# Merging the two softmax maps of a differential pair before they are transposed

## What is computed

```
def differential_attention(q1, q2, k1, k2, v, lam):
    ...
        s1 = jnp.where(causal, jnp.einsum('bqhd,bkhd->bhqk', qa, k1).astype(jnp.float32), -jnp.inf)
        s2 = jnp.where(causal, jnp.einsum('bqhd,bkhd->bhqk', qb, k2).astype(jnp.float32), -jnp.inf)
        attn = jax.nn.softmax(s1, axis=-1) - lam * jax.nn.softmax(s2, axis=-1)
        return jnp.einsum('bhqk,bkhe->bqhe', attn.astype(v.dtype), v)
    ...
o_d = rmsnorm(o_d, diff_norm) * (1.0 - lambda_init)
```

## Time and profile before

| | value |
|---|---|
| median of 3 runs | 2049.18 us (2048.17 to 2049.33) |
| profiled execution | 2048.13 us, its span 2046.2 us |
| busy share of the span | PE 99%, PEld 83%, DVE 79%, ACT 49%, POOL 3% |
| granted TensorE clock | 0.999 of full speed over the span |
| DMA | 376.64 MB, mean 184 GB/s |

### The profile page before, as it was taken

One profiled execution on the slowest core, in us unless ns is written; L12 is line 12 of the kernel. 1 busy time (PEld: TensorE's weight loads), 2 busy tenths in 40 slices (PEclk: granted clock), 3 DMA queues, 4 the chain that ended last, 5 costly groups with the idle time before them and its releaser, 6 DMA issues.

```text
span 2046.2 us, 26929 instructions
## 1 busy us (share of the span) xinstructions
PE 2035.4 (99%) x9638; PEld 1693.0 (83%) x9638; DVE 1619.2 (79%) x2701; ACT 1003.5 (49%) x1192; POOL 67.9 (3%) x87
## 2 busy tenths in 40 slices
PE   9999999999999999999999999999999999999998
PEld 7888888888888888888888889888888888888887
DVE  7888767888887866787888888758888888777887
ACT  5445554444544455454454446355444544665443
POOL 0000100000000010000001000010000000020000
PEclk9999999999999999999999999999999999999999
DMA  6754544555475453465547554234555654434553
GB/s 234 285 189 165 191 147 157 211 200 186 184 257 201 168 197 147 149 213 198 185 167 257 188 185 164 85 123 185 187 198 185 218 196 178 175 141 170 191 197 111
DMA packets 54335, 376.64 MB, mean 184 GB/s; under 512 B 6560, under 2 KB 6704, under 8 KB 9584
## 3 DMA queue, kind: packets, MB, share of 16 engines
q1 hardware_dynamic: 51264, 364.67, 49.3%
q0 software_dynamic: 2560, 10.55, 1.6%
q10 hardware_dynamic: 432, 0.33, 0.0%
HBM read 374.47 MB, written 1.05 MB: 184 GB/s over the span
## 4 chain that ended last, share of the span: by engine, by line
PE 98%; DVE 1%; ACT 1%; issue 0%; DMA 0%; POOL 0%; POOLq 0%; SPq 0%; DVEq 0%; ACTq 0%
PE bank L1654 30%; PE bank L1656 30%; PE bank L1655 30%; PE bank L1663 1%; PE bank L2096 1%; PE bank L2104 1%; PE bank L1877 1%; PE bank L2174 0%; PE bank L1851 0%; PE bank L2175 0%; PE bank L2176 0%; PE bank L1886 0%; DVE w_lo L937 0%; PE bank L1897 0%; PE bank L1899 0%
## 5 line engine op out<-in xcount | busy, mean ns | idle before, releaser
L937 DVE TENSOR_TENSOR w_lo<-w_raw,w_hi 128x2048 fp32r<-128x2048 f32 x344 | 787.5, 2292 | 185.0 <-ACT w_hi L465 116.3
L1654 PE MATMUL bank<-w_hi,xt_hi 128*128 128x512 f32 x1888 | 744.6, 394 | 1.6 <-DVE w_lo L937 1.0
L1656 PE MATMUL bank<-w_hi,xt_lo 128*128 128x512 f32 x1888 | 736.0, 390 | 0.0
L1655 PE MATMUL bank<-w_lo,xt_hi 128*128 128x512 f32 x1888 | 735.2, 389 | 0.0
L994 DVE STREAM_TRANSPOSE mix<-hid 32x128 f32<-32x128 f32 x1408 | 425.8, 302 | 18.3
L1654 PEld LDWEIGHTS bank<-w_hi,xt_hi 128*128 128x128 f32 x1888 | 354.7, 188 | 75.9 <-issue 2.9
L1656 PEld LDWEIGHTS bank<-w_hi,xt_lo 128*128 128x128 f32 x1888 | 354.4, 188 | 74.8
L1655 PEld LDWEIGHTS bank<-w_lo,xt_hi 128*128 128x128 f32 x1888 | 354.8, 188 | 71.2 <-issue 0.2
L465 ACT ACTIVATE w_hi<-w_raw 128x2048 fp32r<-128x2048 f32 x176 | 335.3, 1912 | 147.5 <-PE bank L1656 139.0
L539 ACT ACTIVATE w_hi<-w_raw 128x2048 fp32r<-128x2048 f32 x168 | 320.8, 1910 | 150.8 <-PE bank L1656 150.8
L1654 PE MATMUL bank<-w_hi,ht_hi 128*128 128x512 f32 x608 | 236.7, 389 | 0.0
(11 more groups left out here) (274 smaller groups left out, 1333.9 us busy)
## 6 DMA issues: line engine op xcount, KB each, us to landing
w_raw<-weights_dram SPq DMA_DIRECT2D x345, 1024.0 KB, 4.8
mix<-a_b_gate_dram POOLq DMA_DIRECT2D x4, 1024.0 KB, 14.9
mix<-a_pool_mean_dram POOLq DMA_DIRECT2D x2, 768.0 KB, 7.8
x<-x_dram SPq DMA_DIRECT2D x4, 256.0 KB, 6.4
w_raw<-weights_dram SPq DMA_DIRECT2D x4, 256.0 KB, 6.1
out_dram<-xn SPq DMA_DIRECT2D x3, 256.0 KB, 2.4
mix<-a_pool_w_dram POOLq DMA_DIRECT2D x2, 256.0 KB, 2.9
mix<-g_ret_dram POOLq DMA_DIRECT2D x1, 512.0 KB, 9.6
```

What stands on the lines that cost most here:

```text
L937: nc.vector.tensor_tensor(w_lo[s][:, :], w_raw[s][:, :], w_hi[s][:, :].bitcast(F32), ALU.subtract).then_inc(lo_done, 1)
L1654: nc.tensor.matmul(out, a_hi, b_hi, start=start, stop=False)
L1655: nc.tensor.matmul(out, a_hi, b_lo, start=False, stop=False)
L1656: return nc.tensor.matmul(out, a_lo, b_hi, start=False, stop=stop)
```

## The change

The two maps of a pair are merged after the exponentials and before the transposes. A new DVE step `merge_pair(r)` forms, in place in the first map, map 2r minus lambda times (row sum 1 / row sum 2) times map 2r+1. There is then one turn, one `take_probs` and one `values` a pair. The remaining scale, one over the first row sum, is applied by ACT when it takes the result out of bank 7: `take_pair` moves from DVE to ACT. The eight maps get four buffers `maps` of their own (in `B`, 1536 columns). The dilated maps keep `probs`, and the counts of turns and products go up by one a pair instead of two.

The orders are rewritten too. In pieces 6 to 9 DVE does both `soft` of a pair, then `w_lo` (`ahead`), then `merge_pair`. ACT does `take_pair` and `square_head` of an earlier pair, both exponentials, then `w_hi` (`ahead`), then `take_probs`. On PE the turn of pair r stands in the hooks (7,0), (8,0), (9,0), (10,0) and its product with the values in (7,1), (8,1), (9,1), (10,1). The scores stay in (5,1), (6,1), (7,1) and (8,1).

```
 ScalarE, dil_diff
+                def take_pair(r):
+                    act.wait_ge(pv_done, g0 + r + 1)
+                    for tt in range(TT):
+                        ins = nc.scalar.activation(d4[:, tt, r], bank[7][:, tt * 256:tt * 256 + P], ACT.Copy, scale=expsum[:, 1, tt, 2 * r:2 * r + 1])
+                    ins.then_inc(o_ready, 1)
...
+                    if 8 <= p < 11:
+                        take_pair(p - 8)
+                        square_head(p - 8)
+                    if 6 <= p < 10:
+                        for m in (2 * (p - 6), 2 * (p - 6) + 1):
+                            exp_map(g0 + m, m, diff_map(m))
                     ahead(n0 + p)
...
-                    for step in steps_of(p, 6, 1):
-                        if 2 <= step < 10:
-                            take_probs(g0 + step - 2)
-                        if step < 8:
-                            exp_map(g0 + step, step)
-                        if step in (5, 7, 9):
-                            square_head((step - 5) // 2)
+                    if 7 <= p < 11:
+                        take_probs(g0 + p - 7)
                     if p == 10:
                         turned_qk(c0 + 2, "cqt", 4, B)
+                        take_pair(3)
                         square_head(3)
 VectorE, dil_diff
-                def take_pair(h):
...
+                def merge_pair(r):
+                    dve.wait_ge(exp_done, g0 + 2 * r + 2)
+                    i = 2 * r
                     link(nc.vector.reciprocal(expsum[:, 1, :, i:i + 2], expsum[:, 0, :, i:i + 2]))
                     second = expsum[:, 1, :, i + 1]
+                    link(nc.vector.scalar_tensor_tensor(out=second, in0=second, scalar=lam[:, 5:6], in1=expsum[:, 0, :, i], op0=ALU.mult, op1=ALU.mult))
+                    for tt, cols in enumerate((slice(0, P), slice(P, 3 * P))):
+                        ins = nc.vector.scalar_tensor_tensor(out=diff_map(i)[:, cols], in0=diff_map(i + 1)[:, cols],
+                                                             scalar=expsum[:, 1, tt, i + 1:i + 2], in1=diff_map(i)[:, cols],
+                                                             op0=ALU.mult, op1=ALU.add)
+                    ins.then_inc(maps_merged, 1)
...
                     if 6 <= p < 10:
-                        soft(g0 + 2 * p - 11, 0.125, B["mask"])
+                        soft_diff(2 * (p - 6))
+                        soft_diff(2 * (p - 6) + 1)
                     if p not in (11, last):
                         ahead(n0 + p)
+                    if 6 <= p < 10:
+                        merge_pair(p - 6)
 TensorE, dil_diff
+                def turn_merged_pair(r):
+                    pe.wait_ge(maps_merged, r + 1)
+                    turn_probs(g0 + r, diff_map(2 * r))
...
-                    if 2 <= step < 10:
-                        turn_probs(g0 + step - 2)
-                    if 0 <= step < 8 and step % 2 == 0:
+                    if step % 2 and 3 <= step < 10:
+                        turn_merged_pair((step - 3) // 2)
+                    if step % 2 == 0 and 0 <= step < 8:
                         diff_scores(step)
-                    if 3 <= step < 11:
-                        diff_values(step - 3)
+                    if step % 2 == 0 and 4 <= step < 11:
+                        diff_values((step - 4) // 2)
```

More of the change, by code:

```diff
@@ L647, in pool_attn @@
                         if step < 8:
-                            exp_map(g0 + step, step)
+                            exp_map(g0 + step, step, probs_of(g0 + step))
                     if p == 13 or p == 16:
@@ L1376, in rotate, with soft_diff, soft_dil @@
                     rope(heads(B[name], w), heads(B["rot"], w), tables[:, 0], tables[:, 1], w).then_inc(qk_ready, 1)
[L1378 to L1381 removed]
+                def merge_pair(r):
+                    dve.wait_ge(exp_done, g0 + 2 * r + 2)
+                    i = 2 * r
                     link(nc.vector.reciprocal(expsum[:, 1, :, i:i + 2], expsum[:, 0, :, i:i + 2]))
                     second = expsum[:, 1, :, i + 1]
[L1384 to L1391 removed]
+                    link(nc.vector.scalar_tensor_tensor(out=second, in0=second, scalar=lam[:, 5:6], in1=expsum[:, 0, :, i], op0=ALU.mult, op1=ALU.mult))
[4 more added lines that the diff above has]
+                    ins.then_inc(maps_merged, 1)
+                def soft_diff(m):
+                    if m >= 4:
+                        dve.wait_ge(pt_done, g0 + m // 2 - 1)
+                    soft(g0 + m, 0.125, B["mask"], diff_map(m))
+                def soft_dil(m):
+                    dve.wait_ge(pt_done, g0 + m + 3)
+                    soft(g0 + 8 + m, DIL_SCALE, B["mask_dil"], probs_of(g0 + 8 + m))
                 def lambda_sums():
@@ L1442, in dil_diff @@
                     for step in steps_of(p, 6, 1):
-                        if step < 8 and step % 2 == 0:
-                            soft(g0 + step, 0.125, B["mask"])
-                        if step in (4, 6, 8, 10):
-                            take_pair((step - 4) // 2)
                         if step in (6, 8, 10):
@@ L1457, in dil_diff @@
                         pair_low(bt0[k], 6, first_half)
-                        soft(g0 + 8, DIL_SCALE, B["mask_dil"])
-                        soft(g0 + 9, DIL_SCALE, B["mask_dil"])
+                        soft_dil(0)
+                        soft_dil(1)
                         pair_low(bt0[k] + 1, 7, second_half)
@@ L1573, in pool_attn @@
                         if step < 8:
-                            soft(g0 + step, 0.125, A["mask"])
+                            if g0 + step >= 2:
+                                dve.wait_ge(pt_done, g0 + step - 1)
+                            soft(g0 + step, 0.125, A["mask"], probs_of(g0 + step))
                         if step == 6:
@@ L2336, in diff_scores, with diff_values, turn_dil @@
                     scores_of_pair(g0 + m, mapped("qa")[:, m // 2], mapped("dkt")[:, m // 2])
-                def diff_values(m):
-                    values(g0 + m, m % 2, 2, [dv[:, tt, (m // 2) * P:(m // 2 + 1) * P] for tt in range(TT)], r0 + m // 2)
+                def turn_merged_pair(r):
+                    pe.wait_ge(maps_merged, r + 1)
+                    turn_probs(g0 + r, diff_map(2 * r))
+                def diff_values(r):
+                    values(g0 + r, 0, 2, [dv[:, tt, r * P:(r + 1) * P] for tt in range(TT)], r0 + r)
+                def turn_dil(m):
+                    pe.wait_ge(exp_done, g0 + 8 + m + 1)
+                    turn_probs(g0 + 4 + m, probs_of(g0 + 8 + m))
                 def dil_scores(m):
@@ L2344, in dil_values @@
                 def dil_values(m):
-                    values(g0 + 8 + m, m % 2, 2, [cv[:, tt, m * P:(m + 1) * P] for tt in range(TT)], r0 + 4 + m // 2)
+                    values(g0 + 4 + m, m % 2, 2, [cv[:, tt, m * P:(m + 1) * P] for tt in range(TT)], r0 + 4 + m // 2)
                 def with_tile(p, tt):
```

66 lines of the change are left out of this document (31 added, 35 removed).

## The result

The changed kernel takes 2052.4 us (median of 20 runs, 2051.8 to 2053.9) beside 2049.1 us of the kernel before (20 runs, 2048.1 to 2049.7). The ratio is 1.0017, interval 1.0012 to 1.0023: 2.5 to 4.7 us slower. Forecast was 2052.1.

The account below looks back on a forecast made before the run. PE bounds the kernel (98% of the chain), but its 4.04 us saving meets 3.96 of holds, plus 0.7 for norms and 2.35 for the port: 2051.1 from the profiled run, 2052.1 us on the median's scale, range 2049.0 to 2055.0.

Parts of the forecast that it names:

- PE's saving: On PE, four turns and four products fewer, 4.48 us, of which at most 4.04 us counts in the time.
- The ring: DVE and ACT wait on each other: merge, both soft, exponential, w_hi, w_lo, 8.54 us a piece; holds PE 3.96 us.
- The merge: On DVE, each merge_pair adds 1.14 us of pitch: reciprocal and small op 0.47, large ops 0.27 and 0.40.
- The norm of pairs 0 and 1: In hook (11,0), PE held 0.7 us because w_hi 12 stands behind take_pair 2 on ACT; hook +0.6 us later.
- The port: POOL's rotation of cq locks DVE out of SBUF during merge 1, which ends 2.35 us late, and PE with it.
- L378 has a wait of its own on POOL: At merge 1, POOL's first 1024-column op waits for L376, so both large merge ops may go ahead of it.
- the first rival: At merge 1, POOL's L378 gets in between merge instructions, 2.4 us more, kernel 2054.5 (with L380 2056.9); chance 0.27.
- The sum: Whole kernel: 2048.13 - 4.04 + 3.96 + 0.7 + 2.35 gives 2051.1, on the median's scale 2052.1 us, +2.95.
- The clock: On PE, a granted clock below 1.00 in a hold of over 2 us would make the forecast wrong.

Follow-up runs that it names:

- experiment 8: Changed kernel with merge_pair ahead of w_lo, w_hi 12 ahead of take_pair 2, and POOL's rotation of cq started by w_lo 9 and 10; 2044.71 us, ratio 0.9981.
- experiment 2: Changed kernel without POOL's rotation of cq, one 8-column instruction in place of the four; 2049.36 us, ratio 1.0001.
- experiment 3: Changed kernel with DVE's merge_pair ahead of the w_lo of its piece, POOL's rotation left in place; 2048.99 us, ratio 1.0002.
- experiment 4: experiment 1 with ACT's take_probs of pieces 7 to 9 ahead of both exponentials and w_hi; 2048.07 us, ratio 0.9997.
- experiment 6: experiment 4 with one more DVE instruction of 128x256 on an unread buffer behind each merge; 2053.32 us, ratio 1.0023.
- experiment 7: experiment 4 with ACT's take_pair 2 and its squares behind w_hi 12 instead of ahead of it; 2047.78 us, ratio 0.9998.
- experiment 5: Changed kernel with POOL's two 1024-column operations waiting until merge 1 is done, the two 512-column ones still meeting it; 2050.05 us, ratio 1.0008.
- experiment 1: Changed kernel with POOL's rotation of cq held back until merge 1 is done, its last instruction until merge 2; 2049.43 us, ratio 1.0003.

## Why the prediction came out, and where it didn't

**PE's saving, 4.04 us: right.** 36 matmuls fewer, and a turn or a product costs what the rows said. In experiment 8 cq's turn stands 3.67 us earlier in the stage than before, with one hold of 0.51 ahead of it; in experiment 2 it stands 0.26 us earlier, with holds of 3.92. Both make 4.18.

**The ring, 8.54 us a piece: right.** The merges start at 1788.96 (pair 0), 1797.47 (pair 1) and later 1809.92 and 1818.50: 8.51 and 8.58 us apart where POOL doesn't come in. Without POOL the three holds are 0.76, 0.93 and 2.23 us, 3.92 in all for 3.96 forecast. Experiments 3, 4 and 6 show that it is a ring: moving PE's meeting point moves the hold, lengthening it by 0.45 lengthens a turn from 8.50 to 8.96, and putting the merge ahead of `w_lo` shortens it to 7.39 us.

**The merge, 1.14 us: right.** The reciprocal starts at 1809.92 and the next step after the merge at 1811.05, 1.13 us. The two large ops take 0.75 together; the slower rate of the Trainium skill ("Vector Engine (DVE) Microarchitecture Reference", section 7) for two SBUF sources that are not bf16 does not show in any undisturbed merge. The sum would have been 1.2 us too high by it.

**The norm of pairs 0 and 1, +0.6 us: mechanism right, size off.** The hold is there (0.65, in experiment 2 0.64), and experiment 7 takes it away in the place named, `w_hi` 12 behind `take_pair` 2. But the forecast's +0.6 also had in it that saving and ring nearly cancel, -0.08, and they left -0.26. So in experiment 2 it makes +0.34 at hook (11,0) (1780.22 to 1823.65, 43.43, against 43.09 before). From there to (11,1) it takes 3.90 instead of 4.08 us, and +0.16 is left.

**The port, 2.35 us: this is the term that failed in size.** It measured 3.95. The mechanism, the place and the first two ops were right, though they cost 1.80 (experiment 5), not 2.35, because the small op waited 0.83 and the next 0.97, the rest of a POOL instruction already under way, where I had put 1.1 and 1.25. What failed is the step "L378 has a wait of its own on POOL, so the two large merge ops may slip in ahead of it". The large ops didn't slip in together: the first waited for L385, and L387 (the former L378), ready by the time that one ended, went in between them. That is the first rival's mechanism, to which the prediction gave a chance of 0.27; its price was 2.4 on top of 2.35, which put the kernel at 2054.5, and it measured 2.15 on top of 1.80. The exclusion itself the Trainium skill states ("SBUF — State Buffer", section "SBUF: two separate sides"), and the trace agrees with it: a DVE op of 2 columns lasts 1.05 us. Which instruction gets in when, only the trace told.

**The sum.** In the stage: 0.16 for ring, norms and saving together, where I had 0.6, and 3.95 for the port, where I had 2.35. That is 4.11, and 4.13 was measured. The forecast of +2.95 lies inside the interval of the timed +3.3, and in part that is luck. Two errors pull against each other in the stage, and the timed difference is 0.8 below that of the stage. These 0.8 us stay open. The profiled execution of the kernel before is one of its fastest (2048.13 us, the fastest of 20 took 2048.12) and that of the changed kernel lies 0.5 above its median; part of that lies ahead of the stage, and what other executions did in it isn't recorded. By the timed figures the port costs 2.5 us (the changed kernel against experiments 1 and 2), by the stage 3.95.

**The clock.** The prediction named a granted clock below 1.00 as something that would make it wrong. It did fall, behind the 3.78 us hold of turn 1. The changed kernel's windows, clock behind POOL's column:

```profile
1799.00:1801.00 2.00, 0.33 (x2) 0.00 (x0) 2.00 (x2) 0.00 (x0) 1.92 (x2) 1.00 0.66 279
...
1804.00:1808.00 4.00, 4.00 (x11) 3.13 (x10) 1.11 (x4) 3.88 (x10) 0.86 (x1) 0.50 0.02 6
...
1809.00:1820.00 11.00, 10.59 (x59) 8.41 (x56) 7.72 (x18) 8.82 (x25) 0.84 (x2) 1.00 0.30 101
```

0.50 is the lower level, 1.2 GHz. From turn 1 to the scores PE needs 5.96 us (1802.68 to 1808.64), in experiment 1 at full clock 3.40: 2.56 us. Yet it cost nothing. `take_probs` 1 was done at 1808.05 only, so values 1 were put back from there to 1809.49, and that 1.4 us came out of the hold ahead of values 2, 0.84 instead of 2.2. PE runs at the ring's pace, and a slow PE that is still ahead of the ring loses nothing. In experiment 1 it fell behind the last hold of the ring. It cost 1.58 us on the way to turn 3; only the hold of hook (11,0) was left to swallow some of that (0.64 us in experiment 2, none in experiment 1), and 1.16 us of the stage remained (48.49 against 47.33).

## What to carry to other kernels

Work taken from the busiest engine gives time only if the loop of hand-overs among the others is shorter than what is left to it: write out that loop's pitch, start to start, before counting the saving. When a step such as the merge, with two SBUF inputs, is put on DVE, look up where GpSimd stands at that moment, down to the single instruction, and look after the small one-input ops next to it too (experiment 6). Count every GpSimd instruction that is ready when a DVE instruction ends, also between two that follow each other without a wait. A GpSimd job with slack can be started by a semaphore of the DVE step behind which DVE reads PSUM or idles. Here that was worth about as much as the whole saving: experiments 3 and 8 differ by 4.33 us in the stage, of which the place of `w_hi` 12 is worth 0.43 by experiment 7.

## What the runs showed of the hardware that I had not expected

- GpSimd gets in between two DVE instructions that have no wait between them: 2622 ns for a 256-column op that takes 474 alone. It also stops the smallest ops, 1.05, 1.43, 1.50 and 2.24 us for ops of 2 columns that take 0.16 to 0.22.
- Not every DVE instruction is stopped, and it doesn't take two SBUF inputs to be stopped. `head_mean_square`, a TENSOR_SCALAR of 2 columns with one SBUF input, took 2.24 us beside GpSimd in experiment 6, and 1.14 in the kernel before (1807.36, beside L380), against 0.16 alone. Other forms with one SBUF input were not stopped: the merge's reciprocal kept its 0.18 us beside L387 in experiment 3 (1799.09), and the row maxima of `soft` their 0.29 and 0.41 beside L389 in the changed kernel (1803.13, 1803.33). What sets these apart stays open.
- The granted clock fell to the lower level in or behind holds of PE of 3.78 us (the changed kernel), 3.23 (experiment 3), 4.78 (experiment 6) and 2.22 us (experiment 1), but not behind 2.23 (experiment 2), 2.25 (experiment 4), 2.21 (experiment 5) and 2.28 us (experiment 7). By the windows of 2 us, the fall came while PE was still held in the changed kernel and in experiment 6, and I estimate 0.7 and 1.4 us after PE had started again in experiments 3 and 1. The length of the hold alone doesn't decide it at 2.2 us; what does stays open. Where it fell without cover it cost 1.6 us on the way to the next turn (4.88 against 3.30).
